# Every third weight unit's low part in the feed-forward stages from an accumulating DMA

## What is computed

```
def swiglu_ffn(h, w_gate, w_up, w_down):
    return (jax.nn.silu(h @ w_gate) * (h @ w_up)) @ w_down

x = x + 0.5 * swiglu_ffn(rms_norm(x, ffn1_norm[l]), w_gate[l], w_up[l], w_down[l])
```

## Time and profile before

| | us |
|---|---|
| median of 3 runs | 2153.8 (2153.43 to 2153.88) |
| span of the profiled execution, first to last instruction | 2149.8 |
| median less that span | 4.0 |

### The profile page before, as it was taken

How to read it: one execution, slowest core, us unless ns; L and a number is a source line. 1 busy time by engine, 2 the same in 40 slices (tenths; PEclk the granted TensorE clock), 3 DMA queues, 4 the chain that set the end, 5 groups by cost and what they waited for, 6 DMA issues and landing times.

```text
span 2149.8 us, 39015 instructions
## 1 busy us (share of the span) xinstructions
PE 2112.0 (98%) x13570; PEld 1799.7 (84%) x13570; DVE 1512.8 (70%) x2382; ACT 1144.4 (53%) x1951; POOL 366.7 (17%) x462
## 2 busy tenths in 40 slices
PE   8999999999999999999999999999999999999998
PEld 7888888888888788888888988888888777868887
DVE  6666976667667966667667767667766787677666
ACT  5455755446456755455455445546545454355445
POOL 1111211112111211112111002111111202301111
PEclk9999999999999999999999999999999999999999
DMA  6655435555555345546556554556565453036653
GB/s 253 197 183 184 147 120 201 197 190 172 198 182 193 119 146 194 197 167 197 197 182 226 187 185 162 181 196 205 208 197 183 152 176 103 14 109 203 197 181 128
DMA packets 104401, 376.70 MB, mean 175 GB/s; under 512 B 11764, under 2 KB 12276, under 8 KB 104180
## 3 DMA queue, kind: packets, MB, share of 16 engines
q1 hardware_dynamic: 104308, 375.42, 52.0%
HBM read 373.29 MB, written 1.05 MB: 174 GB/s over the span
## 4 chain that ended last, share of the span: by engine, by line
PE 86%; DVE 7%; ACT 4%; issue 1%; POOL 1%; DMA 1%; SPq 0%; DVEq 0%; POOLq 0%; ACTq 0%
PE bank L939 27%; PE bank L943 14%; PE bank L188 13%; PE bank L189 13%; PE bank L190 13%; DVE w_lo L182 2%; ACT act L478 1%; PE bank L1222 1%; ACT w_hi L175 1%; DVE act L588 1%; PE bank L2215 0%; PE bank L388 0%; PE bank L2205 0%; DVE x L573 0%; ACT work L440 0%
## 5 line engine op out<-in xcount | busy, mean ns | idle before, releaser
L939 PE MATMUL bank<-act,w_hi 128*128 128x512 f32 x2816 | 704.4, 392 | 4.1 <-DVE work L884 2.2
L939 PEld LDWEIGHTS bank<-act,w_hi 128*128 128x128 f32 x2816 | 514.7, 188 | 107.9 <-DVE act L588 4.2
L799 DVE TENSOR_TENSOR w_lo<-raw,w_hi 128x1024 fp32r<-128x1024 f32 x432 | 502.8, 1219 | 4.3 <-issue 1.0
L790 ACT ACTIVATE w_hi<-raw 128x1024 fp32r<-128x1024 f32 x432 | 425.0, 1050 | 2.3
L943 PEld LDWEIGHTS bank<-act,w_lo 128*128 128x128 f32 x2816 | 384.1, 190 | 27.7
L943 PE MATMUL bank<-act,w_lo 128*128 128x256 f32 x2816 | 392.5, 282 | 0.0
L890 DVE TENSOR_TENSOR work<-bank,work 128x256 f32<-128x256 f32 x176 | 74.6, 424 | 376.8 <-ACT work L820 376.8
L182 DVE TENSOR_TENSOR w_lo<-raw,w_hi 128x1024 fp32r<-128x1024 f32 x248 | 294.6, 1219 | 57.3 <-ACT w_hi L175 57.2
L851 POOL TENSOR_TENSOR work<-work,rb 128x256 f32<-128x256 f32 x176 | 129.6, 737 | 1037.9 <-DVE work L884 1037.9
L188 PE MATMUL bank<-w_hi,g_hi 128*128 128x512 f32 x704 | 277.0, 394 | 0.9
L189 PE MATMUL bank<-w_lo,g_hi 128*128 128x512 f32 x704 | 275.9, 392 | 0.0
(11 more groups left out here) (286 smaller groups left out, 2206.3 us busy)
## 6 DMA issues: line engine op xcount, KB each, us to landing
raw<-w_dram SPq DMA_DIRECT2D x680, 512.0 KB, 4.4
work<-rows_dram SPq DMA_DIRECT2D x13, 512.0 KB, 6.1
work<-rrows_dram SPq DMA_DIRECT2D x5, 512.0 KB, 4.0
x<-x_dram SPq DMA_DIRECT2D x2, 512.0 KB, 3.8
out<-x SPq DMA_DIRECT2D x4, 256.0 KB, 2.0
work<-work SPq DMA_DIRECT2D x2, 504.0 KB
work<-g_dram SPq DMA_DIRECT2D x1, 640.0 KB, 9.7
work<-dist_dram SPq DMA_DIRECT2D x2, 256.0 KB, 4.9
```

Of the source, the lines that this page charges most:

```text
L790: nc.scalar.activation(c.w_hi[:, n % RING, :], c.raw[:, n % RING, :], ACT.Copy).then_inc(c.hi_ready, 1)
L799: nc.vector.tensor_tensor(c.w_lo[:, n % RING, :], c.raw[:, n % RING, :], c.w_hi[:, n % RING, :].bitcast(F32), ALU.subtract).then_inc(c.lo_ ...
L939: nc.tensor.matmul(bank[:, :], c.w_hi[:, slot(m), k * P:(k + 1) * P], c.act[:, k, :, :], start=k == 0, stop=False)
```

## The change

In each feed-forward stage the units 6, 9, 12, ... 63 (every third one, the up unit of steps 2 to 21 in the usual start) are "lent". For such a unit ScalarE makes two conversions in place of one: first `w_lo` = the rounded value of -`raw`, then `w_hi` as before. VectorE leaves the unit out. GpSimd waits for `hi_ready` of the unit and, between its two multiplications of step t (in the `late` start behind the second silu multiplication), issues a DMA of 128x1024 that adds `raw` onto `w_lo`. It lands on one of two new semaphores, `ffn_x0` and `ffn_x1`, in turn. TensorE, before it uses the low part, and SyncE, before it loads into the raw slot, wait for that landing in place of `lo_ready`, and `lo_ready` is counted without the lent units. SyncE's first six loads of a stage now stand ahead of its loop. The part `w_lo` that the DMA leaves is not rounded to TensorE's form by the transfer.

Beside it, the start's semaphores are merged: the identity and the first gains share one, and the constants and the remaining columns (429 KB) share one, so whoever waited for one of a pair now waits for both.

```diff
+    LENT = range(6, 3 * FT, 3)
+    c.lent += [first + m for m in LENT]
+    arrived = c.marks("ffn_", {"x0": 16 * len(LENT) // 2, "x1": 16 * len(LENT) // 2})
...
     def sync(sp):
-        with sp.Fori(0, count // RING) as i:
+        for m in range(RING):
+            lo_there(sp, None, m)
+            n = first + RING + m
+            sp.dma_start(c.raw[:, n % RING, :], c.dram["w"][n, :, :]).then_inc(c.landed[n % RING], 16)
+        with sp.Fori(0, count // RING - 1) as i:
             for j in range(RING):
-                n = first + RING + j
-                sp.wait_ge(c.lo_ready, i * RING + (n - RING + 1))
+                n = first + 2 * RING + j
+                lo_there(sp, i, RING + j)
...
+            if m in LENT:
+                nc.scalar.activation(c.w_lo[:, n % RING, :], c.raw[:, n % RING, :], ACT.Copy, scale=-1.0)
             nc.scalar.activation(c.w_hi[:, n % RING, :], c.raw[:, n % RING, :], ACT.Copy).then_inc(c.hi_ready, 1)
...
     def lo_units(dve, i, ms):
         for m in ms:
             n = first + m
+            if m in LENT:
+                continue
...
+    def lend(pool, i, t):
+        m = 3 * t + 3
+        n = first + m
+        pool.dma_start(c.w_lo[:, n % RING, :].bitcast(F32), c.raw[:, n % RING, :],
+                       accum_op=ALU.add).then_inc(arrived[f"x{m // 3 % 2}"].sem, 16)
+
     def pool_step(pool, i, t):
+        m = 3 * t + 3
+        if m in LENT:
+            pool.wait_ge(c.hi_ready, first + m + 1 if i is None else i * RING + (first + m + 1))
         scale_gate(pool, i, t)
+        if m in LENT:
+            lend(pool, i, t)
         scale_silu(pool, i, t)
...
         if late:
             for t in range(2):
                 scale_gate(pool, None, t)
-            for t in range(2):
-                scale_silu(pool, None, t)
+            scale_silu(pool, None, 0)
+            pool.wait_ge(c.hi_ready, first + LENT[0] + 1)
+            scale_silu(pool, None, 1)
+            lend(pool, None, 1)
...
-    s = c.marks("start_", {"ident": 16, "gain": 16, "const": 16, "cols": 16, "x0": 16, "x1": 16})
+    s = c.marks("start_", {"ident": 32, "const": 32, "x0": 16, "x1": 16})
```

## The result

| | before | after |
|---|---|---|
| median of 4 runs, us | 2153.61 (2152.12 to 2153.88) | 2234.57 (2230.52 to 2238.84) |
| ratio | 1 | 1.0374, 95% interval 1.0359 to 1.0389 |
| span of the profiled execution, us | 2149.8 | 2237.0 |

The change makes the kernel slower by 3.7%, 81 us. The forecast was 2169.5 with a range from 2156 to 2205: the sign was right, the size was not, and the time is outside the range.

A forecast was written before the change was run, and what follows sets the result against it. The prediction took TensorE, full in the feed-forward loops, as the bound. It added 15.7 us of stage-start waits and a 4.0 us run-to-profile distance to the 2149.8 us span: 2169.5 us, with a range from 2156 to 2205.

The forecast's parts named there:

- What VectorE gives up and ScalarE takes on: Over 160 lent units VectorE sheds 186 us of differences and ScalarE gains 160 us of conversions; both worth 0 us.
- GpSimd's issue: Issuing the transfer between GpSimd's two multiplications is covered, up to four times 0.74 us: 0 us.
- The merged semaphores: At the kernel's start GpSimd's two roots also wait for the 429 KB of columns, with 2.7 us left: 0 us.
- The stage starts: TensorE's waits for the first lent unit: 6.3 us at six starts, 9.4 at two others, together 15.7 us.
- The landing time: Transfer from issue to landing: 6.0 us, a median load's 4.4 plus 1.56 for a second pass over the bytes.
- In the loop 6.0 is under 8.3: 0 us: In loop steps the 6.0 us landing fits the 8.3 us between issue and TensorE's use, so costs 0 us.
- The loads behind it: SyncE's load into the lent slot waits for the transfer; 5.7 us for a load taking 4.4, so 0 us.
- B: Rival, no slower: landing within 3.4 us at the two tight starts, total 2154 to 2158 us; chance 0.10.
- A: Rival, short landing of 3.5 to 4.9 us: only the two other starts cost, total 2158 to 2161; chance 0.17.
- C: Rival, DMA engines become the bound in the loop: 2230 us at 0.4 us over, 2330 at 1 us; chance 0.18.
- engines full: In the loop, each microsecond a transfer occupies the DMA engines from 3.4 us on is paid in 160 steps.
- mild form: Landing above 8.3 us makes TensorE wait every second loop step: 0.5 us late is 40 us, beside 34 at starts.

The follow-up runs named there:

- e8_noneg: The changed kernel without ScalarE's negative conversion, transfers and waits unchanged: 2234.86 us, ratio 1.0396.
- e3_early: The changed kernel with GpSimd issuing the transfer ahead of its gate multiplication (at the late start ahead of the second silu multiplication): 2178.79 us, ratio 1.0114.
- e9_none: The changed kernel with no unit lent, only the merged start semaphores and SyncE's first six loads ahead of its loop: 2153.14 us, ratio 0.9996.
- e1_first: The changed kernel with only unit 6 of each stage lent, 8 transfers in place of 160: 2167.75 us, ratio 1.0064.
- e10_no6: The changed kernel with units 9, 12, ... 63 lent and unit 6 not, 152 of 160 transfers: 2225.84 us, ratio 1.0339.
- e2_plain: The changed kernel with the transfers as plain copies of raw onto w_lo, without the addition: 2174.26 us, ratio 1.0098.
- e6_half: The changed kernel with every sixth unit lent (6, 12, ... 60), 80 transfers in place of 160: 2171.19 us, ratio 1.0081.
- e5_both: The changed kernel with both the early issue of e3_early and the changed load order of e4_order: 2299.29 us, ratio 1.0688.
- e12_no63: The changed kernel with the last lent unit of each stage, 63, left to VectorE again, 152 transfers: 2224.23 us, ratio 1.0332.
- e7_cols: The changed kernel with each transfer covering 512 of the 1024 columns, 256 KB: 2176.92 us, ratio 1.0106.
- e4_order: The changed kernel with SyncE's load that waits for the landing put last of its three: 2198.18 us, ratio 1.0196.

## Why the prediction was wrong, and where it was right

**What VectorE gives up and ScalarE takes on: right.** VectorE's busy time is 1333.6 us (about 1327 forecast), ScalarE's 1303.1 (1305), and neither is worth anything: e8_noneg takes 150 us of ScalarE's work away and changes no time.

**GpSimd's issue: right.** It takes 0.88 us, 1.02 at the most, between nothing and the bounds that the forecast took as covered. The silu multiplication beside it takes 1005 ns at the mean in place of the 0.73 us of the earlier trace rows. Both are covered; e3_early shows that the second order of the two is worth nothing as engine time: the issue takes GpSimd as long there (0.89 us), and the steps are back.

**The merged semaphores: right,** 0 us (e9_none).

**The stage starts: right in sum, by other parts.** The forecast was 15.7 us, the starts cost 17.7, and e1_first and e10_no6 show them to be a cost of their own. The two `late` starts cost 9.8 us (9.4 forecast), the six others 7.9 (6.3). The first wait of the first stage and that of a `late` stage:

```profile
25.34 1.02 POOL L889 DMA_DIRECT2D w_lo<-raw  x1
...
31.30 1.22 PE L982 MATMUL bank<-act,w_lo 128*128 128x256 f32 x8 [0.68 <-DMA w_lo<-raw]
...
519.93 0.93 POOL L889 DMA_DIRECT2D w_lo<-raw  x1
...
524.59 0.80 PE L193 MATMUL bank<-w_hi,g_hi 128*128 128x512 f32 x1 [3.12 <-DMA w_lo<-raw]
```

At the ordinary start the stall is 0.68 us against 1.05: the landing is 5.9 against 6.0, and the cover is 5.3 (25.34 to 30.62) against 4.95. At the `late` start the landing is 4.6, with no load issued in the 4.6 us before it, so TensorE waits 3.12 us in place of 4.7; but then it works at 1.2 GHz for 3.1 us, which is about 1.6 more. The start is 4.8 us longer than before in this trace, and that it is near the forecast's 4.7 is luck. The term that the forecast did not have is the clock behind a wait. One ordinary start, the fourth stage's, lost 3.7 us instead of about 1, with a stretch of half clock too.

**The landing time, "I take this one, because the transfer runs beside loads": near at the ordinary starts, wrong in its form.** It was taken as one number, 6.0 us, everywhere. At the six ordinary starts it is 5.6 to 6.5, and over all transfers 4.6 to 10.4, with 7.2 at the median. With no load near it is 4.6, that is the plain copy's 2.9 at the least in e2_plain and about the 1.5 us by which the data take longer (0.200 x 2237.0 / 160 = 2.8 us against 0.096 x 2171.5 / 160 = 1.3). The second pass over the bytes is real. Collectives: The Full Stack, of the Trainium skill (Part 3), has an adding DMA read two sources and move half as much; the trace agrees, with 328 ns for a packet against 159. DMA: Bandwidth & Descriptors, of the Trainium skill (Anatomy of one DMA), has a formula that gives 3.2 us for such a DMA, an estimate; measured are 4.6 at the least, and with a plain copy 2.9 at the least and 5.2 at the median, so the estimate is near only for a plain copy with little ahead.

**"In the loop 6.0 is under 8.3: 0 us": this step failed.** It cost 53.4 us, and 4.0 more at unit 63. A median was held against a cover, where the spread decides: a quarter of the transfers take more than 8.2 us to their last packet. e3_early shows it from the side of the cover (about 2.2 us longer, and 52 of the 53 us are gone, with a median landing of 7.8), e6_half from the side of the landing (at most 6.3 us, and all of it gone).

**"The loads behind it ... 0 us, with 1.3 us of cover": this step failed too,** and it feeds the first. A load was counted at its median of 4.4 us after the landing. But the two loads queued behind it are released at the same moment, and the next transfer is due at about the same time. So the next transfer stands behind a burst or a load behind a transfer, and ScalarE, in order, hands the delay on. Three loads of 1.6 and the transfer's 2.8 make 7.6 us of engine time, and with the begin of 1.45 us 9.05, an estimate from these rows; the longest landing is 10.4, and the rest stays unexplained. The forecast had what was needed for such a sum: three loads of 1.56, two passes of 3.1, and the 1.5 us by which the shortest load's landing, 3.1, exceeds its engine time. That is 9.3 us, above the cover of 8.3. It checked each queue by itself.

Of the order in which the engines serve two queues the rows show both forms: packets of the two in turn (0.7 to 0.35 from 72 to 75.5 us of e5_both), and a transfer that begins only when the loads issued ahead of it are nearly done (114.7 for an issue at 109.62); the loads issued at 118.97 likewise begin only at 122.6, behind the transfer of 117.93. The Trainium skill, DMA: Bandwidth & Descriptors (Queues, rings and completion order), has each engine take the queues in turn, packet by packet; the first form agrees, the second is not explained by it, and no run here tells what holds a queue back.

**The rivals.** B did not come. The landing of A, 3.5 to 4.9 us, came only at the two `late` starts (4.6), and not its time. Of C the form "engines full" (3.4 us, from which each further microsecond is paid) is not what binds: with 2.8 us they are not full, and e3_early has a share of 0.89 in a stretch in which TensorE loses 1.2 us of 162. Its mild form, a landing above the 8.3 us and a wait in some of the steps, is what happened: it was priced at 40 us beside 34 at the starts, which would be 2228, and the changed kernel has 53 beside 18, and 16 more that no case had. It was given a part of 0.18 and mostly left out of the range; and it was tied to a long latency of its own, where the cause is the waiting behind loads.

**Around the stages: missing, 16.2 us.** The forecast followed the queued loads only inside the loop. At the end of a stage the same queue of SyncE carries the next stage's rows. e12_no63 gives 13 of the 16 back, 4.0 of them the use of unit 63. It is a cost beside that of the steps: e2_plain, e3_early and e7_cols lose at most 5 us in the steps and still 13 to 17 around the stages.

**What stays open.** For the steps, Q is borne out by e3_early, e6_half and e10_no6, and missed its figures in e4_order and, by far, in e5_both, so it does not yet tell what a new order of the loads will do. What exactly decides whether a stage runs clean wasn't settled (in e4_order the two of the `late` start do, in one trace); nor whether the 3.2 us left around the stages in e12_no63 are unit 60's. That the bursts are what makes a transfer late is read from the order of time and the times of the loads; the runs show only that a longer cover or fewer transfers end both.

## What to carry to other kernels

Hold the longest landing, not the median one, against the cover of a transfer, and add up what stands in front of it: the loads that one landing releases at once, times their engine time, and here those issued up to 1.5 us behind it too. The cover that was short showed in every fourth step only, so one step that looks untouched proves nothing. When a transfer's landing becomes what an in-order load queue waits for, everything behind it in that queue gets a new price, also the loads of the next stage. Where TensorE is full, a wait of it is paid in full and can cost more than its length (about 4.7 us for 3.1 here), so the first question to work moved off a side engine is not what it takes but how late it may be.

## What the chip showed beside that

- An adding transfer on chip takes 328 ns of an engine for a packet of 4096 bytes at the median (339 in e6_half), a plain one 159 (e2_plain), so 2.8 us and 1.3 us of all 16 engines for 512 KB.
- From GpSimd's issue to the first packet it took 1.45 us with no load near, and up to 5.3 us beside loads. Loads issued just behind the transfer ran ahead of it.
- Half the bytes (256 KB) made the median landing only 0.2 us shorter, 7.0 in place of 7.2.
- GpSimd's issue of an adding DMA takes 876 ns, of a plain one 591, and the multiplication right behind the adding one takes 1.03 us in place of 0.74.
- A single wait of TensorE of 1.8 us in a full stream (at 821.6 to 823.3) was followed by 3.4 us at half the clock.
